# Three splits and evacuations moved ahead in ScalarE's and VectorE's order in a hybrid-layer kernel

## Time and profile before

| | |
|---|---|
| median of 3 runs | 1540.25 us (1540.24 to 1541.58) |
| the profiled execution's own time | 1541.66 us |
| its span | 1539.9 us |
| TensorE busy | 1493.7 us (97%), 7367 matmuls |
| VectorE, ScalarE, GpSimd busy | 798.9, 577.7, 657.6 us |
| mean granted TensorE clock | 0.988 |
| DMA | 160.29 MB, mean 104 GB/s |

### The profile page before, as it was taken

The page is one execution under the profiler, slowest core; times in us unless marked ns, Lnnn a source line. Parts: engine busy times, 40 slices in busy tenths (PEclk is TensorE's granted clock), DMA queues, the critical chain, the costliest instruction groups (busy, mean ns, idle before and its releaser), DMA issues.

```text
span 1539.9 us, 21806 instructions
## 1 busy us (share of the span) xinstructions
PE 1493.7 (97%) x7367; PEld 1191.9 (77%) x7367; DVE 798.9 (52%) x1261; ACT 577.7 (38%) x951; POOL 657.6 (43%) x315
## 2 busy tenths in 40 slices
PE   8999999999999999999999999998999999999997
PEld 6768667788888888887767687665887888888887
DVE  5372384652443435864895605674546565654121
ACT  5412673432323223322982325563223232322222
POOL 4333554444444444433344345443443444444442
PEclk9999999999999999989999999999999999999999
DMA  5434211454545555423324234210332333333332
GB/s 155 131 109 124 84 56 54 131 172 152 174 152 170 164 161 171 126 69 94 91 71 102 69 92 76 39 38 21 94 96 69 100 98 100 95 95 89 100 89 93
DMA packets 285179, 160.29 MB, mean 104 GB/s; under 512 B 44931, under 2 KB 272771, under 8 KB 285115
## 3 DMA queue, kind: packets, MB, share of 16 engines
q1 hardware_dynamic: 283566, 156.31, 35.4%
q10 hardware_dynamic: 1548, 3.15, 0.6%
HBM read 156.78 MB, written 5.80 MB: 106 GB/s over the span
## 4 chain that ended last, share of the span: by engine, by line
PE 47%; issue 34%; POOL 12%; DVE 3%; ACT 2%; DMA 1%; POOLq 0%; SPq 0%; DVEq 0%; ACTq 0%
PE ps L2052 13%; PE ps L2054 13%; PE ps L2053 13%; POOL WL L650 12%; PE ps L2536 2%; PE ps L2547 1%; PE ps L2560 1%; PE ps L2289 1%; PE ps L2406 1%; PE ps L2363 1%; PE ps L2349 1%; DVE UL L1703 0%; DMA Wraw<-in_w_in 0%; DVE actL L1648 0%; ACT LP L948 0%
## 5 line engine op out<-in xcount | busy, mean ns | idle before, releaser
L650 POOL TENSOR_TENSOR WL<-Wraw,WH 128x1024 fp32r<-128x1024 f32 (+2 forms) x239 | 572.9, 2397 | 802.8 <-ACT WH L772 802.8
L772 ACT ACTIVATE WH<-Wraw 128x1024 fp32r<-128x1024 f32 (+2 forms) x239 | 246.3, 1031 | 745.1 <-PE ps L2054 719.8
L2052 PE MATMUL ps<-actH,WH 128*128 128x512 f32 x1256 | 503.5, 401 | 12.8 <-POOL WL L650 7.1
L2054 PE MATMUL ps<-actH,WL 128*128 128x512 f32 x1256 | 492.0, 392 | 0.0
L2053 PE MATMUL ps<-actL,WH 128*128 128x512 f32 x1256 | 491.7, 391 | 0.0
L2052 PEld LDWEIGHTS ps<-actH,WH 128*128 128x128 f32 x1256 | 237.7, 189 | 78.5 <-issue 13.8
L2054 PEld LDWEIGHTS ps<-actH,WL 128*128 128x128 f32 x1256 | 237.3, 189 | 51.0
L2053 PEld LDWEIGHTS ps<-actL,WH 128*128 128x128 f32 x1256 | 237.9, 189 | 50.1 <-issue 2.9
L2052 PE MATMUL ps<-UH,WH 128*128 128x512 f32 (+1 forms) x598 | 232.5, 389 | 8.3 <-POOL WL L650 3.9
L2054 PE MATMUL ps<-UH,WL 128*128 128x512 f32 (+1 forms) x598 | 229.3, 383 | 0.0
L2053 PE MATMUL ps<-UL,WH 128*128 128x512 f32 (+1 forms) x598 | 229.2, 383 | 0.0
(11 more groups left out here) (287 smaller groups left out, 1437.2 us busy)
## 6 DMA issues: line engine op xcount, KB each, us to landing
Wraw<-in_w_ff SPq DMA_DIRECT2D x64, 512.0 KB, 4.1
Wraw<-in_w_in SPq DMA_DIRECT2D x56, 512.0 KB, 4.0
wada<-in_w_ada SPq DMA_DIRECT2D x64, 384.0 KB, 4.4
Wraw<-in_w_up SPq DMA_DIRECT2D x44, 512.0 KB, 3.7
Wraw<-in_w_down SPq DMA_DIRECT2D x16, 448.0 KB, 3.6
Wraw<-in_w_proj_rnn SPq DMA_DIRECT2D x16, 320.0 KB, 3.2
Wraw<-in_w_proj_mla SPq DMA_DIRECT2D x8, 512.0 KB, 3.8
Wraw<-in_w_out SPq DMA_DIRECT2D x8, 512.0 KB, 3.8
```

Source lines behind the costliest of these rows:

```text
L650: nc.gpsimd.tensor_tensor(WL[slot][:, 0:kts, :], Wraw[slot][:, 0:kts, :], WH[slot][:, 0:kts, :].bitcast(F32), ALU.subtract).then_inc(s_lo, 1)
L772: A(WH[slot][:, 0:kts, :], Wraw[slot][:, 0:kts, :], ACT.Copy).then_inc(s_hi, 1)
L2052: MM(o, wh, ah, start=first, stop=False)
L2054: return MM(o, wl, ah, start=False, stop=last)
```

## The change

It moves work in the fixed order of two engines; what is computed stays the same.

1. ScalarE makes the high part of `gQK`'s weight 2 right after the Ln (line 867), ahead of its wait for VectorE's log-sigmoid; step 0 of the loop no longer makes it.
2. In the last round of the recurrence, `rnn_rest` gets a second hook, `middle()`, between Tanh and the square roots: there ScalarE makes the high part of `gGate`'s weight 12 and evacuates block 10. `between()` then makes the high part of weight 13 (number 5 counted from the round's first), which round 5 no longer makes.
3. VectorE evacuates the first block of `gPR` (`pr_first(0)`) between the low parts of the query latents and the norm of the key latents, and the second one where the loop began; the loop runs three rounds in place of four.

```diff
--- before.py
+++ after.py
@@ -865,6 +865,7 @@
             own.done(A(T[1][:], ps[:, 2, :], ACT.Abs, bias=vec[:, VEC["gla_b_a"]:VEC["gla_b_a"] + 1]))
             own.done(A(T[1][:], T[1][:], ACT.Exp, scale=-1.0))
             A(T[1][:], T[1][:], ACT.Ln, bias=ones[:, 0:1]).then_inc(S("gla_log"), 1)
+            high(gQK, 2, gQK.n0 + 2, landed(gQK, 2, 0, 4))
             act.wait_ge(S("gla_logsig"), 1)
             A(gla_decay, T[0][:], ACT.Exp, scale=1.0 / B_TAU).then_inc(S("gla_alpha"), 1)
             act.wait_ge(S("gla_cleared"), 4)
@@ -917,9 +918,9 @@
                       ).then_inc(S("gla_on_act"), 1)
 
             for n in range(2 * PAIRS):
-                if n + 2 < 2 * PAIRS:
+                if 0 < n < 2 * PAIRS - 2:
                     high(gQK, 2 + n % 4, gQK.n0 + n + 2, landed(gQK, 2 + n % 4, n // 4, 4))
-                else:
+                elif n:
                     high(gV, n + 2 - 2 * PAIRS, gV.n0 + n + 2 - 2 * PAIRS, landed(gV, n + 2 - 2 * PAIRS))
                 if n == 0:
                     gla_values_out()
@@ -1105,7 +1106,7 @@
                 A(T[j][:], ps[:, 2 + 2 * j, :], ACT.Sigmoid, bias=bias_at("b_gate_a_2", t, j)).then_inc(S("rnn_sig"), 1)
                 A(T[2 + j][:], ps[:, 3 + 2 * j, :], ACT.Sigmoid, bias=bias_at("b_gate_x_2", t, j)).then_inc(S("rnn_sig"), 1)
 
-            def rnn_rest(t, between):
+            def rnn_rest(t, middle, between):
 
                 marks = []
                 for j in range(2):
@@ -1114,6 +1115,7 @@
                         act.wait_ge(S("rnn_low"), t + (j - 1))
                     A(rA[:, j, :], T[j][:], ACT.Exp).then_inc(S("rnn_a"), 1)
                     A(rTh[:, j, :], T[j][:], ACT.Tanh, scale=-1.0).then_inc(S("rnn_tanh"), 1)
+                middle()
                 for j in range(2):
                     act.wait_ge(S("rnn_m2"), t + (j + 1))
                     A(rTh[:, j, :], rTh[:, j, :], ACT.Sqrt).then_inc(S("rnn_mult"), 1)
@@ -1142,7 +1144,7 @@
                     for j in range(2):
                         if not ahead and j == 0:
                             high(gLat, 0, gLat.n0, landed(gLat, 0))
-                        elif ahead and not (j == 0 and after_rnn):
+                        elif ahead and not (after_rnn and (j == 0 or isinstance(i, int) and i == RT // 2)):
                             high(gGate, 2 + j, 2 * i + (gGate.n0 + 2 + j), landed(gGate, 2 + j, i))
                         if rnn or j or not after_rnn:
                             evac(i, j, dst, t0)
@@ -1153,12 +1155,16 @@
                         if after_rnn or isinstance(i, int) and i == RT // 2:
                             rnn_high(2 * i - 2, j)
 
+                    def middle():
+                        if last_rnn:
+                            high(gGate, 4, 2 * i + (gGate.n0 + 4), landed(gGate, 4, i))
+                            evac(i + 1, 0, gM, KT)
+
                     def between():
-                        high(gGate, 4, 2 * i + (gGate.n0 + 4), landed(gGate, 4, i))
-                        if last_rnn:
-                            evac(i + 1, 0, gM, KT)
+                        n = 5 if last_rnn else 4
+                        high(gGate, n, 2 * i + (gGate.n0 + n), landed(gGate, n, i))
                     if rnn:
-                        rnn_rest(2 * i, between)
+                        rnn_rest(2 * i, middle, between)
                 return body
             peeled(act, KT // 2, gate_round(gR, 0, rnn=True))
             for i in range(KT // 2, RT // 2):
@@ -1838,6 +1844,11 @@
                     g = gR[:, ds(2 * i + j, 1), :].rearrange("p a t -> p (a t)")
                     V.tensor_tensor(g, ps[:, gPR.bank(j), :], g, ALU.mult).then_inc(s_ev, 1)
 
+            def pr_first(j):
+
+                dve.wait_ge(s_mm, gPR.n0 + 2 * j + 2)
+                V.tensor_tensor(gR[:, j, :], ps[:, gPR.bank(j), :], gR[:, j, :], ALU.mult).then_inc(s_ev, 1)
+
             dve.wait_ge(S("pos_loaded"), 16)
             c1 = 6.28125
             c2 = float(np.float32(2 * math.pi - c1) - np.float32(2 * math.pi - c1) % np.float32(2.0 ** -20))
@@ -1871,6 +1882,9 @@
             for k in range(QT):
                 low("nq", k, lambda k: actL[:, k, :], lambda k: actH[:, k, :], None)
             dve.wait_ge(*N("nq", "low", QT))
+            dve.wait_ge(S("gate_evacuated"), 2 * KT)
+            dve.wait_ge(s_ev, gRope.b0 + 1)
+            pr_first(0)
             for k in range(KVT):
                 norm_scaled("nkv", k, lambda k: lat[:, QT + k, :], lambda k: vcol("kv_norm_g_2", k), Vf[:])
 
@@ -1882,8 +1896,8 @@
             dve.wait_ge(S("krot_ready"), 3)
             for k in range(KVT):
                 low("nkv", k, lambda k: actL[:, QT + k, :], lambda k: actH[:, QT + k, :], None)
-            dve.wait_ge(S("gate_evacuated"), 2 * KT)
-            repeat(dve, KT // 2, pr_round)
+            pr_first(1)
+            repeat(dve, KT // 2 - 1, lambda i: pr_round(i + 1))
 
             for b in range(1, 2 * TB, 2):
                 dve.wait_ge(*((S("m_valued"), b + 1) if b < 2 * TB - 1 else (s_mm, gVal.n0 + KVT)))
```

## The result

| | before | after |
|---|---|---|
| median, six runs each on one chip | 1541.44 us (1540.24 to 1542.84) | 1533.80 us (1528.48 to 1535.94) |
| ratio, 95% interval | | 0.9943 [0.9932, 0.9953] |
| the profiled execution's own time | 1541.66 us | 1532.12 us |
| its span | 1539.9 us | 1530.3 us |
| mean granted TensorE clock | 0.988 | 0.990 |

The kernel is faster, by about 9 us and not 12.3, and 1533.8 lies above the range of 1525.4 to 1532.0. Its six runs spread over 7.5 us and those of the kernel before over 2.6, but over 6 to 9 us, 0.4 to 0.6%, in the larger sets further down: more than the 0.3% within which most executions of a kernel agree.

A forecast was written before the change was run, and what follows sets the result against it. TensorE was taken to bound the kernel; gains of 3.4 (query/key), 3.9 (last recurrence round) and 5.0 us (recurrent projection) sum to 12.3, taking the median from 1540.25 to 1528.0 us, range 1525.4 to 1532.0.

The forecast's parts named there:

- Part 3: First recurrent-projection block: early evacuation removes block 2's wait and the half clock behind it; 5.0 us, from 4.2 to 5.4.
- Part 2: Last recurrence round: gate block 12 starts 2.75 us earlier, half clock 1.6 gone, block 13 0.5 late; 3.9 us.
- Part 1: Query/key products: weight 4's load issued earlier, so block 4 starts at 83.6, not 87.2; 3.4 us, from -0.2 to 5.7.
- The even share of queues: Rival: weight 4's load gets equal bytes beside the DRAM transfer, block 4 doesn't wait, 2.1 us more gain: 1525.9; chance 0.10.
- VectorE's cover: VectorE's lead in the query/key loop hides later decays and low-part stalls; 0.2 us given back, two stalls 3.8 if gone.
- The transfer inside DRAM itself starts no later: Query/key phase: its issue waits only for the log-sigmoid, done at 66.59, when the new copy is over.
- a pause of 2.1 us stays: Before query/key block 4: TensorE still waits 2.1 us for weight 4, with full clock assumed behind it.
- the first rival: The clock falls all the same before query/key block 4, costing 1.6 us: 1529.6; chance 0.25.
- nothing behind these places holds a time of its own: After the three changed places TensorE runs on at full clock, 1.00 over 84 to 650 us, so gains stay.
- The load that lands no earlier: Rival: query/key weight 4 lands as late as before, or lost VectorE cover takes the 3.4 us: 1531.4; chance 0.10.
- The clock as a budget: Rival: less TensorE rest brings half clock in the dense run from 84 to 650 us: 1543.0; chance 0.02.
- Delays that come back at the next norm: Rival: VectorE's and ScalarE's delays in recurrence and recurrent projection return, saving only part of one pause: about 1538; chance 0.03.

The follow-up runs named there:

- part 3 alone: Kernel before, with only the first recurrent-projection block evacuated ahead of the key latents' norm: median 1537.61 us, ratio 0.9968.
- parts 2 and 3: The change without its early high part of query/key weight 2, against the kernel before: median 1534.67 us, ratio 0.9963.
- the second execution: Traced execution of the unedited changed kernel from its second measurement, against the kernel before: that measurement's median 1530.88 us, ratio 0.9933.
- part 1 alone: Kernel before, with only query/key weight 2's high part made ahead of the log-sigmoid's wait: median 1540.95 us, ratio 0.9992.
- the later transfer: Changed kernel with the 3 MB transfer inside DRAM issued three blocks later, behind weight 4's high part: median 1530.84 us, ratio 0.9926 to the kernel before.
- the third: Traced execution of the unedited changed kernel from its third measurement, against the kernel before: that measurement's median 1531.98 us, ratio 0.9928.
- the pause filled: Changed kernel with 16 idle matmuls in the pause before query/key block 4: median 1529.51 us, ratio 0.9916 to the kernel before.
- the two held kernels: Small matmuls in four untouched pauses: kernel before, 1542.50 us; with weight 2's early high part and 16 matmuls before block 4, 1540.61 us.

## Why the prediction was right or wrong

**Direction, places and most mechanisms held.** Each of the three waits went, and the next thing late was the one named.

- *Part 3, 5.0 us*: 5.1 in the three traces of the change and in that of part 3 alone, 4.6 in that of parts 2 and 3, 4.9 by the ratio.
- *Part 2, 3.9 us*: 3.4 in the traces, 3.1 by the ratio. Copy, table load, sigmoid and table load came in the order and the times named. The earlier start with the half clock was put at 4.35 and measured 4.2. Block 13's delay was put at 0.5; the offsets lose 0.8 in two steps, 0.3 at block 13 and 0.5 at block 14. The bank is free at 804.65 + 0.60 = 805.25 and block 13 starts at 805.39, 5.79 us after block 12; block 14 then waits for its weight, which ScalarE makes behind the second copy of the recurrence, and this was not in the sum.
- *Part 1, block 4 at 83.6*: 84.17, 83.30, 84.03 and 83.48 in the four traces, 83.75 on average. A part of this closeness is luck: these executions were between 0.1 us behind and 0.6 ahead before place 1, and on the scale of before block 4 starts at 83.8 to 84.1, 3.1 to 3.4 us earlier and not 3.6. The load took 11.4 to 11.7 us, where 11.2 were assumed.
- *The even share of queues* has fallen: 3.7 us alone, 11.6 beside the transfer. What has fallen is the equal share of bytes. The Trainium skill's rule of turns by whole packets of several descriptors (DMA: Bandwidth & Descriptors, "Queues, rings and completion order") doesn't say how many bytes a turn has, and the prediction was wrong to take equal bytes from it: near-equal counts (245 and 233) of 0.5 and 2 KB fit turns of equal counts as well. How the queues take turns is not shown here.
- *VectorE's cover* was there, but thin. In the second execution the offset was 3.9 us at block 4 and 3.9 at 190 us, so nothing was given back; in part 1 alone a wait of 0.27 us was, where 0.2 was assumed. Copies met low parts all the same, as these rows of VectorE's timeline in the profile of after show:

```profile
74.05 1.85 DVE L1537 COPY gKc<-T 128x16 f32<-128x16 f32 x1
...
81.98 2.18 DVE L1537 COPY gKc<-T 128x16 f32<-128x16 f32 x1
```

  GpSimd's low parts ran from 73.45 to 75.86 and from 81.78 to 84.12. A copy of this shape took 0.17 us elsewhere in that timeline. The stalls are those that the Trainium skill's exclusive lock (SBUF — State Buffer, "SBUF: two separate sides") leads to. VectorE's lead over the sums took them up; with the later transfer one of them cost block 4 the 0.56 us.

- *"The transfer inside DRAM itself starts no later"* was wrong: ScalarE's queue issues it with the Exp, 1.2 us later. By the traces it changed little, as the load is beside it for its whole length either way; no run separates it.

**The step that failed** is "a pause of 2.1 us stays" before block 4, at full clock behind it. It rested on the pause of some 1.8 us in the earlier trace rows that kept the clock. There were 2.26 to 2.54 us of pause, and the clock fell in two of the three executions of the change that were traced (two of four with part 1 alone) and took 1.4 to 1.5 us. That is the first rival (1529.6), mixed half and half into the forecast. The sample was not a safe one either: that pause, 1.95 us in the timeline, kept the clock in the kernel before and lost it in the second execution of the change, where it cost 1.6 us, and also in the third, in part 3 alone and with the pause filled. TensorE before, then in the second execution:

```profile
1054.79 0.64 PE L2560 MATMUL ps<-PT_even,Vtok 128*64 128x512 f32 x1 [1.95 <-ACT PT_even L1221]
```

```profile
1042.13 1.11 PE L2574 MATMUL ps<-PT_even,Vtok 128*64 128x512 f32 x1 [1.95 <-ACT PT_even L1227]
```

Beside it, the sum took the half-clock stretches of one profiled execution as fixed: "nothing behind these places holds a time of its own", with 1.00 over 84 to 650. Outside the three places the profile of after has one more stretch near 191 (1.5 us) and a shorter one near 654 (a gain of 1.1), the second execution one more near 1042 (1.6), the third two more (near 191 and 1046, 1.5 and 1.7 us). That these come by chance is shown by the three traces of one program.

**The sum.** The mean of the three measured gains is 10.1 us (8.8, 10.3, 11.1) against 12.3. The half-and-half loss behind block 4 takes 0.75, part 2's size 0.5 and block 4's later start 0.2, which leaves 10.9. The 0.8 that remains is within what the three differ by, and the runs don't settle it; the stretches outside the places are of that size. Nor is part 1's worth settled: 1.2 alone, 2.1 by the two held kernels' ratios (with a filler that overran) and 5.4 on top of parts 2 and 3. As for the time itself, 1533.8 is 5.8 above the forecast: 3.5 us is the gain of the first measurement (8.8 for 12.3), 1.2 is the base (1540.25 then, 1541.44 in this comparison), and 1.1 the difference between its ratio and its medians. So the failed step is the smaller part of the 5.8, and for a good part of the rest the cause stays open. The two repeated measurements, 1530.88 and 1531.98, lie within the range.

**Rivals.** The load that lands no earlier: block 4's times exclude it. The clock as a budget: the second execution, with all three parts in it, has no half-clock stretch between block 4 and 649 us. Delays that come back at the next norm: the offsets of 9.5 us behind place 3 stay to the end in the profile of after, and what the other traces lose there they lose at half clock near 1042 to 1050.

## What to carry to other kernels

Work out a gain at its place, from who is late next, but then ask of every pause that the change leaves or makes whether the clock may fall behind it, and count half of that loss where like pauses did both. One pause that kept the clock in one profile is no evidence that the next will. Half-clock stretches of one profile are a sample, not a property of the kernel: read the clock of two or three executions before a difference of 2 us is explained. A filler must be shorter than the pause that it fills; where a load makes the pause, moving the transfer that runs beside it takes most of the pause away, though here it gained only 0.3 us by the ratios, too little to tell.

## What the hardware showed that was not expected

- The same pause both kept and lost the clock: 1.41 us near 191 (20 matmuls in 2.87 or 4.00 us), 1.95 us near 1044, 2.50 to 2.54 us before block 4, 3.0 us before block 12, and the 3.12 us before block 2 of the merge, behind which the window 1068 to 1073 of parts 2 and 3 has 1.00 and 1076 to 1080 of the kernel before 0.62. What decides was not found.
- The 512 KB load took 3.7 us alone and 11.6 beside a 3 MB transfer inside DRAM whose packets are four times as large.
- A half-clock stretch between two blocks, of which the second waits for a load, cost nothing: block 4 starts at 87.21 with it and at 86.79 without, in an execution that was 0.9 us ahead.
- Out of a wait of VectorE for GpSimd (a copy of 1.82 us and not 0.17) came one of TensorE, 0.56 us, through the evacuation queued behind the copy.
